# A hybrid decoder with product-key experts: the low half of the weighted activations moves from VectorE to GpSimd, with four activation buffers and a new spread of the gathered rows

## The reference

```python
def peer_ffn(xn, w_q, k1, k2, u, v):          # for each token:
    q = xn @ w_q                              # 8 heads, 2 halves of 128
    v1, i1 = top_k(q[:, :, 0] . k1, 16)
    v2, i2 = top_k(q[:, :, 1] . k2, 16)
    top_s, pos = top_k(v1[:, None] + v2[None, :], 16)
    ids = the 16 chosen of 128 * 128 experts  # per head
    g = softmax(top_s)
    act = u[ids] . xn
    return sum(g * gelu(act) * v[ids])
```

## Time and profile before

| What | us |
|---|---|
| median of 3 runs (lowest to highest) | 3242.73 (3241.24 to 3245.43) |
| profiled execution, its own time | 3249.34 |
| its span | 3247.5 |
| TensorE busy | 3202.2 |
| VectorE busy | 2597.5 |
| GpSimd busy | 1191.4 |

### The profile page before, as it was taken

How to read it: one execution, slowest core, us unless ns; L and a number is a source line. 1 busy time by engine, 2 the same in 40 slices (tenths; PEclk the granted TensorE clock), 3 DMA queues, 4 the chain that set the end, 5 groups by cost and what they waited for, 6 DMA issues and landing times.

```text
span 3247.5 us, 54682 instructions
## 1 busy us (share of the span) xinstructions
PE 3202.2 (99%) x19694; PEld 3000.9 (92%) x19694; DVE 2597.5 (80%) x4972; ACT 1508.2 (46%) x2298; POOL 1191.4 (37%) x789
## 2 busy tenths in 40 slices
PE   8999999999999999999999999999999999999998
PEld 7878888999999999999988788889999999999998
DVE  6654449999998889999866544499999888999997
ACT  5553233477773333333345532334777633333333
POOL 1000014335435656555300000143454456665552
PEclk9999999999999999999999999999999999999999
DMA  4214422589999999999821143225999999999996
GB/s 148 78 53 143 142 90 91 194 326 386 400 398 399 357 389 390 413 409 416 310 91 66 53 156 130 97 100 189 346 391 393 405 393 370 390 398 417 415 411 258
DMA packets 232172, 893.29 MB, mean 275 GB/s; under 512 B 23856, under 2 KB 69088, under 8 KB 184128
## 3 DMA queue, kind: packets, MB, share of 16 engines
q1 hardware_dynamic: 112912, 455.25, 37.2%
q0 software_dynamic: 99024, 355.98, 27.8%
q10 hardware_dynamic: 20064, 79.91, 6.2%
HBM read 809.57 MB, written 81.48 MB: 274 GB/s over the span
## 4 chain that ended last, share of the span: by engine, by line
PE 63%; issue 14%; DMA 12%; DVE 8%; POOL 2%; ACT 1%; SPq 0%; DVEq 0%; POOLq 0%; ACTq 0%
PE bank L1506 18%; PE bank L1508 18%; PE bank L1507 18%; DMA act_in<-act_d 9%; PE bank L1815 4%; DVE h L1383 4%; DVE w_lo L1411 2%; POOL lo L568 1%; PE bank L1624 1%; PE bank L1661 1%; DMA rows<-in_u_rows,ids 1%; PE bank L1642 1%; DMA raw<-in_stream 1%; DVE lo L983 1%; ACT hi L626 1%
## 5 line engine op out<-in xcount | busy, mean ns | idle before, releaser
L626 ACT ACTIVATE hi<-raw 128x2048 fp32r<-128x2048 f32 (+2 forms) x338 | 620.6, 1836 | 692.9 <-PE bank L1508 396.1
L1506 PE MATMUL bank<-xT_hi,hi 128*128 128x344 f32 (+1 forms) x2688 | 918.7, 342 | 2.1 <-DVE xT_lo L1033 1.7
L1508 PE MATMUL bank<-xT_hi,lo 128*128 128x344 f32 (+1 forms) x2688 | 905.1, 337 | 0.0
L1507 PE MATMUL bank<-xT_lo,hi 128*128 128x344 f32 (+1 forms) x2688 | 900.3, 335 | 0.0
L983 DVE TENSOR_TENSOR lo<-raw,hi 128x2048 fp32r<-128x2048 f32 (+2 forms) x320 | 698.4, 2183 | 183.1 <-ACT hi L626 180.9
L1506 PE MATMUL bank<-w_hi,hi 128*128 128x344 f32 x2048 | 662.3, 323 | 19.2 <-DVE w_lo L1411 18.6
L1507 PE MATMUL bank<-w_lo,hi 128*128 128x344 f32 x2048 | 655.0, 320 | 0.0
L1508 PE MATMUL bank<-w_hi,lo 128*128 128x344 f32 x2048 | 654.0, 319 | 0.0
L615 POOL DMA_INDIRECT rows<-in_v_rows,ids x256 | 426.1, 1665 | 301.6 <-DVE h L1383 248.2
L1506 PEld LDWEIGHTS bank<-xT_hi,hi 128*128 128x128 f32 x2688 | 504.2, 188 | 32.3 <-issue 5.9
L1508 PEld LDWEIGHTS bank<-xT_hi,lo 128*128 128x128 f32 x2688 | 504.4, 188 | 25.3
(11 more groups left out here) (258 smaller groups left out, 4108.8 us busy)
## 6 DMA issues: line engine op xcount, KB each, us to landing
raw<-in_stream SPq DMA_DIRECT2D x352, 1024.0 KB, 7.6
gate_in<-gate_d SPq DMA_DIRECT2D x96, 384.0 KB, 12.4
act_d<-act_s ACTq DMA_DIRECT2D x92, 352.0 KB, 6.3
gate_d<-gate_s ACTq DMA_DIRECT2D x22, 1472.0 KB, 9.6
act_in<-act_d SPq DMA_DIRECT2D x92, 352.0 KB, 10.0
gate_d<-gate_s ACTq DMA_DIRECT2D x22, 576.0 KB, 13.7
gate_in<-gate_d SPq DMA_DIRECT2D x32, 256.0 KB, 9.6
rows<-in_u_rows,ids POOLq DMA_INDIRECT x256, 10.0
```

The costliest lines, as they stand in the source:

```text
L626: act.activation(hi[s][:, 0:n], raw[s][:, 0:n], ACT.Copy).then_inc(hi_done, 1)
L1506: pe.matmul(dst, a_[0], b_[0], start=first, stop=False)
L1507: pe.matmul(dst, a_[0], b_[1], start=False, stop=False)
L1508: return pe.matmul(dst, a_[1], b_[0], start=False, stop=last)
```

## The change

`w_lo` is made by GpSimd in place of VectorE, for all 64 down chunks of each layer. For this GpSimd's gathers are written by steps: in step q it issues those that `rows_by(q - 1)` and the seven slots allow, and then makes `w_lo` of q + 1. The spilled activations go through four buffers, `act_in` and `act_k`, and their load is issued two chunks earlier. The G stage gets 72 row operations in place of 96, and the steps behind it have three shares: 41 for a U chunk, 28 for a kept one, 24 for a V chunk (before 16 for U and 13 for the others). The first gate loads stand beside chunks 48 and 49 in place of 50 and 51, and four steps at which gelus and weighings of the gathered tokens stand are moved along with the rows.

```diff
@@
-ROWS_IN_G = 96
+ROWS_IN_G = 72
-E_GELU, E_WEIGH = 12, 14
+E_GELU, E_WEIGH = 14, 16
@@
-SHARED = 2
+SHARED, ACT_BUFS = 2, 4
-GATES_AT = {50: (0, 0), 51: (0, 2), 52: (1, 0), 53: (1, 1), 54: (1, 2), 55: (1, 3),
+GATES_AT = {48: (0, 0), 49: (0, 2), 52: (1, 0), 53: (1, 1), 54: (1, 2), 55: (1, 3),
-GATES_FROM, V_FROM = 50, 80
-ROW_GELU_AT, WEIGH_ROWS_AT = 70, 74
-UP_SHARE, DOWN_SHARE, ROWS_END = 16, 13, 2 * C_U - 2
+GATES_FROM, V_FROM = 48, 80
+ROW_GELU_AT, WEIGH_ROWS_AT = 69, 73
+UP_SHARE, KEPT_SHARE, DOWN_SHARE, ROWS_END = 41, 28, 24, 2 * C_U - 2
@@ rows_by
-    shares = [UP_SHARE if x in UP_OF else DOWN_SHARE for x in range(FIND_STEPS + G_STEPS, ROWS_END)]
+    shares = [UP_SHARE if x in UP_OF else KEPT_SHARE if DOWN_OF[x] < KEPT else DOWN_SHARE for x in range(FIND_STEPS + G_STEPS, ROWS_END)]
@@ sync
-                def load_act(j, s):
-
+                def load_act(v, x):
+
+                    j, s, b = v * ACT_BUFS // 2 + x // 2, x % 2, x % ACT_BUFS
                     wait_alone(sp, act_out[s], 16 * (l * ACT_PAIRS + j) + 16, sp_passed)
-                    sp.wait_ge(w_done, done + 2 * j + s + 1)
-                    sp.dma_start(act_in[:, s].rearrange("p i t -> p (i t)"), act_d[2 * j + s - KEPT]).then_inc(act_ld[s], 16)
+                    sp.wait_ge(w_done, done + ACT_BUFS * v + x - ACT_BUFS + 1 + CR)
+                    sp.dma_start(spilled_acts(b).rearrange("p i t -> p (i t)"), act_d[ACT_BUFS * v + x - KEPT]).then_inc(act_ld[b], 16)
@@ v_loads
-                        if not (isinstance(v, int) and v * V_CHUNKS + c < KEPT):
-                            load_act(v * V_CHUNKS // 2 + c // 2, c % 2)
+                        if not last or c + 2 < V_CHUNKS:
+                            load_act(v, c + 2)
@@ gpsimd (the body of the old loop over n is now fetch(n))
-                for n in range(ROW_OPS):
-
+                def fetch(n):
@@
+                def weigh_lo(c):
+                    pool.wait_ge(w_hi_done, l * C_V + c + 1)
+                    acts = acts_of(c, c % 2) if c < KEPT else spilled_acts(c % ACT_BUFS)
+                    pool.tensor_tensor(w_lo[:, c % 2], acts, w_hi[:, c % 2].bitcast(F32), ALU.subtract).then_inc(w_done, 1)
+
+                n = 0
+                for q in range(FIND_STEPS, 2 * C_U - 1):
+                    while n < min(ROW_OPS, max(0, rows_by(q - 1)) + NR):
+                        fetch(n)
+                        n += 1
+                    if q + 1 in DOWN_OF:
+                        weigh_lo(DOWN_OF[q + 1])
@@ vector
-                def weigh_lo(c):
-                    s, k = c % 2, l * C_V + c
-                    dve.wait_ge(w_hi_done, k + 1)
-                    dve.tensor_tensor(w_lo[:, s], acts_of(c, s), w_hi[:, s].bitcast(F32), ALU.subtract).then_inc(w_done, 1)
@@
-                    if q + 1 in DOWN_OF:
-                        weigh_lo(DOWN_OF[q + 1])
                     while n < rows_by(q):
```

More of the change, by code:

```diff
@@ L452, in build @@
         gate_ld = [sem(f"gate_ld{s}") for s in range(2)]
-        act_ld = [sem(f"act_ld{s}") for s in range(2)]
+        act_ld = [sem(f"act_ld{b}") for b in range(ACT_BUFS)]
         prod_done, w_hi_done, w_done, y_ps = (
@@ L472, in acts_of, with spilled_acts, acts_loaded @@
         def acts_of(k, s):
-            return (act_k, act_s, act_in)[k % SPAN // 2][:, s] if isinstance(k, int) and k < KEPT else act_in[:, s]
+            return (act_k, act_s, act_in)[k % SPAN // 2][:, s]
+        def spilled_acts(b):
+            return (act_in, act_k)[b // 2][:, b % 2]
+        def acts_loaded(l, c):
+            b = c % ACT_BUFS
+            first = KEPT + (b - KEPT) % ACT_BUFS
+            return act_ld[b], 16 * (l * len(range(first, C_V, ACT_BUFS)) + (c - first) // ACT_BUFS + 1)
         @block.sync
@@ L617, in _ @@
                                             ).then_inc(rows_in[N % NR], 16)
+                def weigh_lo(c):
[9 more added lines that the diff above has]
+                        weigh_lo(DOWN_OF[q + 1])
+                assert n == ROW_OPS
         @block.scalar
@@ L936, in _, with weights_hi @@
                             store_gates(q // PER_SLICE)
-                def weights_hi(c, s):
+                def weights_hi(c, s, b):
                     act.wait_ge(prod_done, l * C_V + c + 1)
@@ L943, in weights_hi @@
                         act.wait_ge(w_used, 2 * (lp + P_V) + c + 1)
-                    act.activation(w_hi[:, s], acts_of(c, s), ACT.Copy).then_inc(w_hi_done, 1)
+                    acts = acts_of(c, s) if isinstance(c, int) and c < KEPT else spilled_acts(b)
+                    act.activation(w_hi[:, s], acts, ACT.Copy).then_inc(w_hi_done, 1)
                 for q in range(FIND_STEPS + G_STEPS, C_V + KEPT):
@@ L952, in _ @@
                     if q + 1 in DOWN_OF:
-                        weights_hi(DOWN_OF[q + 1], (q + 1) % 2)
+                        weights_hi(DOWN_OF[q + 1], (q + 1) % 2, DOWN_OF[q + 1] % ACT_BUFS)
                     if q in UP_OF:
@@ L958, in _, with v_steps @@
                             store_act(UP_OF[q] // 2, q % 2)
[L960 to L968, removed]
+                def v_steps(v, first, end):
+                    for x in range(first, end):
+                        ahead(lp + P_V + v * ACT_BUFS // 2 + x // 2, x % 2)
+                        weights_hi(v * ACT_BUFS + x + 1, (x + 1) % 2, (x + 1) % ACT_BUFS)
+                v_steps(KEPT // ACT_BUFS, KEPT % ACT_BUFS, ACT_BUFS)
+                with act.Fori(KEPT // ACT_BUFS + 1, C_V // ACT_BUFS - 1) as v:
+                    v_steps(v, 0, ACT_BUFS)
+                v_steps(C_V // ACT_BUFS - 1, 0, ACT_BUFS - 1)
                 if l + 1 < DEPTH:
@@ L1400, in weigh_step @@
                     else:
-                        dve.wait_ge(act_ld[s], 16 * (l * ACT_PAIRS + (c - KEPT) // 2 + 1))
+                        dve.wait_ge(*acts_loaded(l, c))
                     dve.wait_ge(gate_ld[v % 2], 16 * GATE_PARTS * (v // 2 + 1))
-                    a_ = acts_of(c, s).rearrange("p i (q t) -> p i q t", t=SLICE)
+                    acts = acts_of(c, s) if c < KEPT else spilled_acts(c % ACT_BUFS)
+                    a_ = acts.rearrange("p i (q t) -> p i q t", t=SLICE)
                     i = 2 * (c % V_CHUNKS)
```

## The result

The changed kernel takes 3326.67 us in the median of 4 runs (3325.06 to 3331.97), the kernel before, on the same chip, 3244.08 (4 runs, 3241.24 to 3250.28): ratio 1.0255, 95% interval 1.0235 to 1.0274. The forecast was 3272 and its range ended at 3306. The direction was right; the size was not.

What follows compares the result with a forecast made beforehand. It took PE's chunk floors as the bound, 35 us above them winnable, with VectorE nearly full. Per layer +2 + 13.6 - 1 = +14.6, both layers +29 on the 3242.7 median: 3272 us, range 3236 to 3306.

Steps and rivals of the forecast that it cites:

- Part 1: `w_lo` on GpSimd takes 1.73 us; VectorE saves 0.80, is shut out for 1.52, net loss 0.72 a chunk.
- free: Rival: VectorE isn't shut out, or GpSimd's turn falls in its pauses; 3221 to 3226 us; chance 0.14.
- Part 2: GpSimd's queue: `w_lo` between gathers, 6.8 to 9.0 us a V chunk; no stall of its own counted for PE.
- convoy: Rival: `w_lo` behind gathers that wait for rows and port; V chunks at 8.3 us; 3316 or 3294; chance 0.17.
- Part 3: Chunks 82 to 126: `act_in` wait goes, VectorE sets 7.80 us a chunk, 351.0 us in all; +2 a layer.
- Part 4: Chunks 52 to 81: VectorE needs 242.9 us, PE 226.3; less a 3.0 us lead, +13.6 us a layer.
- Part 5: Chunks 43 to 51: 32.9 MB exceed DMA's ceiling, partly covered by rows landed ahead; stall 6 us, was 7.0; -1 a layer.

Runs made afterwards that it cites:

- new_rows_wlo_dve: Changed kernel with `w_lo` back on VectorE and GpSimd's gathers in one plain loop, so new rows, gates and buffers alone: 3292.65 us.
- spare_sub: Kernel before, `w_lo` on VectorE, plus an extra GpSimd subtraction in the V chunks whose result nobody reads: 3299.82 us.
- lo_first: Changed kernel with GpSimd's subtraction placed before the gathers of its step, not behind them: 3400.99 us.
- four_buffers: Kernel before with only the four activation buffers and earlier loads; `w_lo` on VectorE, old rows and gates: 3246.08 us.
- thin_v: Kernel before with the four activation buffers and earlier loads, and 116 rows in chunks 82 to 126 in place of 121: 3233.91 us.
- thin_v2: Kernel before with the four activation buffers and earlier loads, and 114 rows in chunks 82 to 126 in place of 121: 3234.22 us.
- half_weights: Changed kernel with `w_lo` on VectorE, gathers in a plain loop, and only half of each weight chunk loaded in steps 48 to 79: 3272.86 us.
- short_rows: Changed kernel with `w_lo` on VectorE, gathers in a plain loop, and VectorE working on 512 of 1024 row columns in steps 43 to 81: 3277.98 us.
- half_both: Changed kernel with `w_lo` on VectorE, plain gather loop, half weight loads (steps 48 to 79) and half-row VectorE work (steps 43 to 81): 3238.98 us.
- spare_copy: Kernel before, `w_lo` on VectorE, plus an extra GpSimd copy of 704 elements in the V chunks, one input instead of a subtraction's two: 3250.04 us.

## Why the prediction was right in direction and wrong in size

**Part 1 (the price of the move) was right.** Forecast: 1.73 us for 704 elements, VectorE shut out for 1.52, net loss 0.72 a chunk. Measured: the shortest `w_lo` on GpSimd takes 1.68 us. In the V stretch the rows take 212.4 us and lo 105.8, in new_rows_wlo_dve, with the same rows, 151.1 and 103.0; so 64.1 us are lost in 45 chunks, 1.42 each. Net, VectorE's busy time rose from 317.23 to 342.59 us, 0.56 a chunk. The Trainium skill's rule in "GPSIMD Engine Reference", section "Key points", that VectorE instructions with two SBUF inputs contend with GpSimd, agrees with the row of 2.72 us. The narrower note in "Advanced Engine Details and Errata", section "VectorE Performance Modes", doesn't cover it. The rival *free* fell. spare_sub shows the price without any wait for the result.

**Part 2 (the queue) held in the V chunks and failed in the kept ones.** The V chunks took 7.73 us each, not GpSimd's 8.3, so *convoy* as I had described it is not what happened, though its 3316 is nearest in number. In the kept chunks "no stall of its own" was wrong: the wait of 3.40 us above is one, and in the changed kernel PE waits for a `w_lo` issued 5.63 us after its `w_hi`, behind two gathers, as well (2.90 us at 1156.95). Not every such wait is the queue's: in new_rows_wlo_dve PE waits at the turns for `w_lo` from VectorE too (3.2, 4.7 and 4.4 us in layer 0). How the 21.4 us split between the queue and VectorE's loss stays open. lo_first shows that the other order costs 74 us more; that the change has the cheaper of these two was luck, since I had priced neither.

**Part 3 (V chunks) was near.** 351.0 forecast, 347.8 measured in both layers. But its cause for the loss before, the wait for `act_in`, was wrong: four_buffers took it away and gained nothing. The gain that pays for `w_lo` in V comes from five rows less (342 us in new_rows_wlo_dve), which I had noted only as "under the ceiling". That bytes set these chunks rests on the late weight chunks and on thin_v; thin_v2 shows that little of it is left below 116 rows.

**Part 4 (chunks 52 to 81) failed by a missing term.** Forecast +13.6 a layer; measured +31.1 and +34.4. Its sum was VectorE's alone. The move of `w_lo` gave 10.5 and 12.3 (the changed kernel against new_rows_wlo_dve), close to it. The other 20.6 and 22.1 are the rows, and this step put DMA at nothing. The term could be made from before: chunks 70 to 75 moved 17.9 MB in 45.57 us, with 17 + 4 gathers issued; 27 in their place are 3.1 MB more, and 21.1 MB at the 415 GB/s of this stage are 50.8 us, 5.2 of the 8 us by which the block became longer. The bound that I gave, +20, had 3 us for late rows and nothing for this. VectorE has its part in the loss of these blocks too, since halving the rows' work gives back nearly as much as halving the weights (the table below), though its busy time in the changed kernel, 43.7 and 48.5 us, is near the 44.2 and 49.6 that I had summed. So what failed beside the missing term is the overlap: I had taken the larger of PE's and VectorE's time, less a lead.

**Part 5 (chunks 43 to 51) failed by a term read as a stall.** Forecast -1 a layer, measured +8.3 both. The DMA summaries of the stage, before and then after:

```profile
DMA packets 8495, 30.19 MB, mean 412 GB/s; under 512 B 812, under 2 KB 2759, under 8 KB 7322
```

```profile
DMA packets 9359, 33.05 MB, mean 406 GB/s; under 512 B 893, under 2 KB 2937, under 8 KB 8199
```

Before, the queues moved 30.2 MB in 73.25 us, 412 GB/s at share 1.02 from end to end. So I now read its 7 us at chunk 51 not as one late load behind four gate loads, but as the whole stage's bytes, paid where the rows in hand ran out; no run took bytes out of this stage of the kernel before. After, 33.05 MB: 2.9 MB more at 407 GB/s are 7.0 us of the 8.3, and new_rows_wlo_dve has 7.3 and 7.7 of it without the subtraction. I had worked out 32.9 MB, but let five rows landed ahead pay for 2.6 of them. Some cover was in both kernels: only 36 of the 40 gathers were issued in the stage (30 before), and still 33 MB moved, since I had left out the stores of `gate_d` (1472 and 576 KB) and a part of the gate loads.

**How bytes and VectorE share the loss.** Over the whole kernel one relief gives 20 or 15 us, both 54. By stages, in us that the profiled execution gained on new_rows_wlo_dve's, both layers together:

| Chunks | half_weights | short_rows | half_both |
|---|---|---|---|
| 43 to 51 | 9.8 | 0.5 | 15.4 |
| U blocks 58 to 63 and 70 to 75 | 14.4 | 12.0 | 26.3 |
| the three kept blocks | -0.8 | -1.2 | 9.6 |

In chunks 43 to 51 less work for VectorE gives nothing by itself, and 5.6 us once bytes are gone too: the bytes come first there. In the other U blocks the two gains simply add up, so both loads cost time. Only in the kept blocks must both go before anything comes back, which is where most of the rest of the 54 lies. A pause costs clock besides. Chunks 51 and 52 of the changed kernel:

```profile
1028.65:1040.22 11.57, 9.38 (x49) 9.12 (x49) 11.51 (x15) 4.66 (x5) 9.35 (x6) 0.85 1.03 416
1040.22:1051.61 11.39, 9.31 (x49) 9.06 (x49) 10.30 (x13) 2.81 (x3) 9.98 (x6) 0.85 0.98 383
```

Each takes 11.4 to 11.6 us for 7.5 of work, of which PE shows 9.3 busy, since a part of it ran at 1.2 GHz, not 2.4, behind the pause before. How the loss of a U block splits between bytes, VectorE and clock for each single chunk stays open.

**The sum of it.** In medians: rows and gates 46.6 (new_rows_wlo_dve less four_buffers), `w_lo` on the kept chunks 21.4, on the spilled ones 12.6, four buffers -1.7: 78.9 together (differences of a chain of medians, so they add up by themselves); the remaining 3.7 of the 82.6 are the difference between the two medians of the kernel before (3247.76 and 3244.08). Without the blocking, parts 4 and 5 had given the rows +1 and -1 a layer.

## What to carry to other kernels

Make the table of bytes for every stage whose load rises, as carefully as that of engine time, and take the total that the trace of before moved in the stage, not a list made by hand: a stage that moves 412 GB/s from end to end, as chunks 43 to 51 did, has bytes to lose before it has a stall to win. Before a limit is relaxed, ask what the second one is: here one relief gave 20 us, the other 15, both 54. Work moved to GpSimd cost VectorE about its own length less 0.26 us, where VectorE's work reads two SBUF operands; count it where VectorE is full. And price the order on GpSimd's queue, stage by stage: a subtraction behind gathers made PE wait, gathers behind a subtraction that waits made the rows late.

## What the chip showed that I had not expected

- A GpSimd copy with one input takes time from VectorE's two-input work too: 0.52 us for 704 elements, against 1.1 for a subtraction with two inputs in the same place (VectorE's busy time in spare_copy and spare_sub). The shortest copy takes 0.78 us, the shortest subtraction there 1.37. The end time moved by 0.13% only.
- GpSimd's subtraction is itself held up by VectorE: 2.88 us on the mean in the V chunks of the changed kernel, where the shortest takes 1.68; it starts while VectorE makes lo.
- With the new rows DMA gave 405 to 416 GB/s over the first and third U blocks at a share of 1.02 or 1.03, but 385 to 388 over the second at 0.99 to 1.01, and with `w_lo` on VectorE 397 to 400 over the V stretches at 0.99 or 1.00, where the weight chunks are late all the same.
